# Sums of the modulation on VectorE, narrow stationary columns, and row norms by step over four tiles

## The reference

```python
# first block
mod = silu(c) @ w_ada + b_ada                     # (1, 6*1024)
shift1, scale1, gate1, shift2, scale2, gate2 = split(mod, 6)
h = rms_norm(x, norm1_w) * (1 + scale1) + shift1
q, k, v, cb, cc, cx, iq, ik, iw = split(h @ w_in)
y = concat(rms_norm(topk_attention(q, k, v, iq, ik, iw)), rms_norm(short_conv(cb, cc, cx)))
x = x + gate1 * (y @ w_out)
h2 = rms_norm(x, norm2_w) * (1 + scale2) + shift2
x = x + gate2 * retrieval(h2)                     # 16,384 single-neuron experts
# second block
x = layer_norm(ALPHA * x + hybrid_mixer(x), ...)  # its projection has 8 columns beta, a (decay)
x = layer_norm(ALPHA * x + expert_layer(x), ...)  # 32 experts, top 2
# third block
x = x + hybrid_layer(rms_norm(x), ...)            # four attention branches and w_out
```

## Time and profile before

| what | value |
|---|---|
| three timed runs | 4040.03, 4041.31, 4035.67 us; median 4040.03 |
| the profiled execution | 4024.92 us, span 4022.9 us |
| busy: TensorE, VectorE, ScalarE, GpSimd | 3259.2, 2388.5, 1419.9, 1257.1 us |
| first mixer's first product to its end | 52.9 to 489.6 us |
| mixers' first product | 2083.39 us |
| routing: last rest, first product | 2857.04, 2857.79 us |
| third block's first product | 3553.57 us |

### The profile page before, as it was taken

The page is one execution under the profiler, slowest core; times in us unless marked ns, Lnnn a source line. Parts: engine busy times, 40 slices in busy tenths (PEclk is TensorE's granted clock), DMA queues, the critical chain, the costliest instruction groups (busy, mean ns, idle before and its releaser), DMA issues. The chain is left out here.

```text
span 4022.9 us, 35798 instructions
## 1 busy us (share of the span) xinstructions
PE 3259.2 (81%) x12074; PEld 2065.8 (51%) x12074; DVE 2388.5 (59%) x4585; ACT 1419.9 (35%) x2251; POOL 1257.1 (31%) x1107
## 2 busy tenths in 40 slices
PE   8999688677666776667678898899399999578888
PEld 5555573222222222222256686677288888456556
DVE  3665474666666666666527646544489889544444
ACT  2323222112221112111114323233378888533443
POOL 0000046777777777777720000000111221100000
PEclk9999799999999999989979998799699999879888
DMA  6233178999999999999952220022599999611111
GB/s 221 66 112 103 49 244 320 355 365 367 359 361 371 361 361 369 371 362 349 371 194 76 59 73 17 27 76 93 199 338 375 373 368 375 226 42 48 32 32 53
DMA packets 421241, 896.43 MB, mean 223 GB/s; under 512 B 38081, under 2 KB 179137, under 8 KB 420418
## 3 DMA queue, kind: packets, MB, share of 16 engines
q0 software_dynamic: 157984, 549.57, 36.5%
q1 hardware_dynamic: 263074, 344.54, 25.3%
HBM read 891.80 MB, written 27.35 MB: 228 GB/s over the span
## 5 line engine op out<-in xcount | busy, mean ns | idle before, releaser
L263 PE MATMUL peer_acc<-peer_vbuf,peer_diag 128*128 128x512 f32 x2048 | 1026.1, 637 | 402.8 <-issue 181.6
L263 PEld LDWEIGHTS peer_acc<-peer_vbuf,peer_diag 128*128 128x128 f32 x2048 | 377.1, 199 | 1049.0 <-issue 897.3
L452 DVE CUSTOM_DVE_ANT_0 peer_junk<-peer_ubuf,firsts_h 128x1024 f32<-128x1024 f32 x512 | 624.7, 1225 | 452.6 <-DMA peer_ubuf<-in_peer_u,peer_experts 336.7
L220 POOL DMA_INDIRECT peer_ubuf<-in_peer_u,peer_experts x512 | 532.7, 1040 | 699.4 <-DVE peer_experts L423 533.8
L228 POOL DMA_INDIRECT peer_vbuf<-in_peer_v,peer_experts x512 | 581.5, 1136 | 230.2 <-issue 125.7
L329 ACT ACTIVATE peer_diag<-all_consts,peer_weights 128x128 f32<-128x128 f32 x512 | 194.5, 398 | 1014.2 <-PE peer_acc L263 469.4
L2985 DVE TENSOR_TENSOR slotted_low<-slotted_raw,slotted_high 128x2048 fp32r<-128x2048 f32 x192 | 434.2, 2289 | 66.1 <-ACT slotted_high L2934 66.1
L2934 ACT ACTIVATE slotted_high<-slotted_raw 128x2048 fp32r<-128x2048 f32 x192 | 365.6, 1920 | 71.1 <-PE slotted_h L2891 51.3
L2752 POOL MEMSET slotted_xg<- 128x4096 f32 x1 | 3.5, 3512 | 774.5 <-POOLq L60 774.5
L2891 PE MATMUL slotted_h<-slotted_high,slotted_xT_high 128*128 128x512 f32 x512 | 205.1, 401 | 6.2 <-DVE slotted_low L2985 4.1
L2891 PE MATMUL slotted_h<-slotted_high,slotted_xT_low 128*128 128x512 f32 x512 | 201.9, 394 | 0.0
(11 more groups left out here) (736 smaller groups left out, 5928.2 us busy)
## 6 DMA issues: line engine op xcount, KB each, us to landing
slotted_raw<-in_moe_w SPq DMA_DIRECT2D x192, 1024.0 KB, 9.2
mixers_raw<-in_w_in SPq DMA_DIRECT2D x56, 512.0 KB, 3.8
firsts_ada_raw<-in_w_ada SPq DMA_DIRECT2D x64, 256.0 KB
third_raw<-in_w_in SPq DMA_DIRECT2D x30, 512.0 KB, 3.7
firsts_raw<-in_w_in SPq DMA_DIRECT2D x28, 512.0 KB, 4.1
firsts_ada_first<-in_w_ada SPq DMA_DIRECT2D x8, 1024.0 KB
peer_s<-in_peer_wq SPq DMA_DIRECT2D x16, 512.0 KB
peer_ubuf<-in_peer_u,peer_experts POOLq DMA_INDIRECT x512
```

The source lines that it names most:

```text
L220: pool.indirect_dma_start(ubuf[:, n % R, :], None, A["peer_u"], bass.IndirectOffsetOnAxis(ap=experts[:, t, m:m + 1], axis=0))\
L263: mm = nc.tensor.matmul(acc[t % 2][j][:, :], diag[:, n % 4, :], vbuf[:, n % R, j * BANK:(j + 1) * BANK], start=(n == t * E), stop=(n == (t ...
L452: nc.vector.tensor_tensor_reduce(junk[:, n % 2, :], ubuf[:, n % R, :], h2[:, t, :], 1.0, 0.0, ALU.mult, ALU.add, act_in[:, t, m:m + 1]).th ...
```

## The change

1. **First mixer, sums.** The 64 matmuls at L687 go. VectorE multiplies each tile of `w_ada` by its column of silu(c) and adds it up (64 operations of 128x512), and one matmul with a matrix of ones sums the partitions, eight in all. Half of the 64 steps have keys from -4 on (2.25 apart), half from 140 on (2.6 apart).
2. **First mixer, plan.** Other periods for the pieces of v, q and k, and the convolution; the two closing pieces of the convolution's part are split off and come earlier, and half 1's products of a tile are cut in two; scores and softmax works have shorter spacing, selection rounds a longer one; the transposes and splits of the tail stand later.
3. **Mixers, ab.** Beta and decay columns are stationary, the 512 tokens move: 24 matmuls in place of 96, the result is copied by ScalarE and turned by four small transposes in the middle of piece 1.
4. **Routing rows.** Ordered by step over the four tiles by a written list; the norm is two operations with two tensor sources each in place of one with one source and two with two; the router's rounding and rest come after the first rows.
5. **Third block's rows.** The same order and norm; the GpSimd addition is gone, VectorE makes `x*ALPHA + ya` and then `+ yb`.

```diff
-                (stationary("v", W[:, 2 * DA:3 * DA], 4) + stationary("q", W[:, 0:DA], 4)
-                 + stationary("k", W[:, DA:2 * DA], 4), 6.9),
+                (stationary("v", W[:, 2 * DA:3 * DA], 4), 9.0),
+                (stationary("q", W[:, 0:DA], 4) + stationary("k", W[:, DA:2 * DA], 4), 6.0),
                 (stationary("cc", W[:, 4 * DA:5 * DA], 4) + stationary("cx", W[:, 5 * DA:6 * DA], 4)
-                 + stationary("cb", W[:, 3 * DA:4 * DA], 4), 11.0),
-                (closing, 5.6)]
+                 + stationary("cb", W[:, 3 * DA:4 * DA], 4), 8.0),
+                (closing[0:2], 8.0), (closing[2:], 5.6)]
...
+            now += {"2": 18.0, "0": 26.0}.get(part_of(part), 0.0)
...
-        ADA_AT, ADA_STEP = 112.0, 2.5
+        FIRST = 32
 
         def ada_key(q):
-            return ADA_AT + ADA_STEP * q
+            return 2.25 * q - 4.0 if q < FIRST else 140.0 + 2.6 * (q - FIRST)
+
+        def ada_acc(j):
+            return (acc_first if j < 4 + FIRST // 8 else acc_last)[:, j % 2, :]
...
-            for q in range(8 * (N_ADA - 4)):
-                yield ada_key(q)
-                j, k = 4 + q // 8, q % 8
-                if q == 0:
+            for j in range(4, N_ADA):
+                yield ada_key(8 * (j - 3) - 1) + 1.5
+                if j == 4:
                     pe.wait_ge(h_low, 2 * NT)
...
-                mm = nc.tensor.matmul(side[j % 2][:, :], c_col[:, k:k + 1].broadcast_to([P, P]), ada_raw[:, q % 2, :],
-                                      start=(k == 0), stop=(k == KD - 1))
+                if j >= 4 + FIRST // 8:
+                    pe.wait_ge(sq_rooted, 2)
+                pe.wait_ge(ada_out, j - 1)
+                pe.wait_ge(ada_used, 8 * (j - 3))
+                nc.tensor.matmul(side[j % 2][:, :], C["ones"], ada_acc(j), start=True, stop=True).then_inc(ada_done, 1)
...
+                    for k in range(KD):
+                        q = 8 * (j - 4) + k
+                        yield ada_key(q)
+                        dve.wait_ge(ada2_in[q % 2], 16 * (q // 2 + 1))
+                        if k == 0:
+                            dve.wait_ge(ada_done, j - 1)
+                            if q == FIRST:
+                                dve.wait_ge(rectified, len(rels))
+                            ins = nc.vector.tensor_scalar(ada_acc(j), ada_raw[:, q % 2, :], c_col[:, k:k + 1], None, ALU.mult)
+                        else:
+                            dve.wait_ge(ada_used, q)
+                            ins = nc.vector.scalar_tensor_tensor(ada_acc(j), ada_raw[:, q % 2, :], c_col[:, k:k + 1], ada_acc(j),
+                                                                 ALU.mult, ALU.add)
+                        ins.then_inc(ada_used, 1)
+                    yield ada_key(8 * (j - 3) - 1) + 4.0
...
-                return starts[IN] + 10.0 + 3.0 * (p - HALF1)
+                return starts[IN + 2] + (-8.0, -4.0, 3.0, 6.0)[p - HALF1]
...
+                    if i == 2:
+                        yield starts[HALF1] + 5.6 * t + 2.8
...
-        REL_AT, REL_STEP = done_key("iw", 0) + 3.0, 1.9
-        PICK_AT, PICK_STEP = REL_AT + REL_STEP * len(rels) + 2.0, 3.2
+        REL_AT, REL_STEP = done_key("iw", 0) + 3.0, 1.35
+        PICK_AT, PICK_STEP = REL_AT + REL_STEP * len(rels) + 2.0, 3.6
...
-                at += (3.6, 4.4, 5.0, 5.6)[t]
+                at += (3.2, 3.6, 4.2, 4.6)[t]
...
+                low_at = half1_key(t) + (11.6, 11.6, 11.6, 7.6)[t]
                 later += [(half1_key(t), 1, t), (half1_key(t) + 2.6, 2, t), (half1_key(t) + 3.2, 3, t),
-                          (half1_key(t) + 7.4, 4, 2 * t), (half1_key(t) + 7.8, 4, 2 * t + 1)]
+                          (low_at, 4, 2 * t), (low_at + 0.3, 4, 2 * t + 1)]
...
+                high_at = half1_key(t) + (9.6, 9.6, 8.6, 7.0)[t]
+                later += [(half1_key(t) + 1.6, 1, t), (half1_key(t) + 2.9, 2, t), (high_at, 3, 2 * t),
+                          (high_at + 0.4, 3, 2 * t + 1)]
...
-                yield half1_key(t) + 6.4 + 0.4 * half
+                yield half1_key(t) + (8.35, 8.35, 6.4, 6.4)[t] + 0.02 * half
...
                     if name == "ab":
-                        for t in range(NT):
-                            for k in range(KD):
-                                for r, (a, b) in enumerate(three_products((xh[:, k, tile(t)], xl[:, k, tile(t)]),
-                                                                          (wh[:, k, :], wl[:, k, :]))):
-                                    mm = nc.tensor.matmul(bank[:, 2 * BH * t:2 * BH * t + 2 * BH], a, b,
-                                                          start=(k == 0 and r == 0), stop=(k == KD - 1 and r == 2))
+                        for k in range(KD):
+                            for r, (a, b) in enumerate(three_products((xh[:, k, :], xl[:, k, :]), (wh[:, k, :], wl[:, k, :]))):
+                                mm = nc.tensor.matmul(bank[0:2 * BH, :], b, a, start=(k == 0 and r == 0),
+                                                      stop=(k == KD - 1 and r == 2))
...
+                                if p == 1:
+                                    pe.wait_ge(ab_copied, 1)
+                                    for t in range(NT):
+                                        tr = nc.tensor.transpose(big[0][:, 2 * BH * t:2 * BH * t + 2 * BH], abT[0:2 * BH, tile(t)],
+                                                                 C["ident"][0:2 * BH, 0:2 * BH])
+                                    tr.then_inc(ab_turned, 1)
...
-        later = [(row_key(t, step), step, t) for t in range(NT) for step in (2, 5, 9, 10)]
+        order = (("mean", 0), ("mean", 1), ("norm", 0), ("mean", 2), ("norm", 1), ("mean", 3), ("norm", 2), ("low", 0), ("low", 1),
+                 ("norm", 3), ("low", 2), ("low", 3), ("low", 4), ("low", 5), ("low", 6), ("low", 7))
+        for i, (what, t) in enumerate(order):
+            yield float(i)
+            if what == "mean":
...
-            elif step == 5:
+            elif what == "norm":
                 dve.wait_ge(rooted, t + 1)
                 if t == 0:
                     dve.wait_ge(rows_loaded, 32)
                 chain(nc.vector.reciprocal(roots[:, t:t + 1], roots[:, t:t + 1]))
-                chain(nc.vector.tensor_scalar(x[:, t, :], x[:, t, :], means[:, t:t + 1], roots[:, t:t + 1], ALU.add, ALU.mult))
-                chain(nc.vector.tensor_tensor(x[:, t, :], x[:, t, :], ob[:, 0, :], ALU.mult))
-                nc.vector.tensor_tensor(x[:, t, :], x[:, t, :], ob[:, 1, :], ALU.add).then_inc(x_ready, 1)
+                chain(nc.vector.scalar_tensor_tensor(x[:, t, :], x[:, t, :], means[:, t:t + 1], ob[:, 0, :], ALU.add, ALU.mult))
+                nc.vector.scalar_tensor_tensor(x[:, t, :], x[:, t, :], roots[:, t:t + 1], ob[:, 1, :], ALU.mult, ALU.add)\
+                  .then_inc(x_ready, 1)
...
-        yield -20.0
+        yield 9.5
...
-        def rows_pool(pool):
...
-                nc.gpsimd.tensor_tensor(ya[:, t, :], ya[:, t, :], yb[:, t, :], ALU.add).then_inc(y_added, 1)
...
+            order = (("add", 0), ("add", 1), ("mean", 0), ("add", 2), ("mean", 1), ("norm", 0), ("add", 3), ("mean", 2), ("norm", 1),
+                     ("second", 0), ("mean", 3), ("norm", 2), ("second", 1), ("low", 0), ("low", 1), ("norm", 3), ("second", 2),
+                     ("low", 2), ("low", 3), ("second", 3), ("low", 4), ("low", 5), ("low", 6), ("low", 7))
+            for i, (what, t) in enumerate(order):
...
+                if what == "add":
+                    dve.wait_ge(y_in[t], 32)
+                    nc.vector.scalar_tensor_tensor(ya[:, t, :], x[:, t, :], ALPHA, ya[:, t, :], ALU.mult, ALU.add)\
+                      .then_inc(y_added, 1)
                     dve.wait_ge(y_added, t + 1)
-                    nc.vector.scalar_tensor_tensor(x[:, t, :], x[:, t, :], ALPHA, ya[:, t, :], ALU.mult, ALU.add)\
-                      .then_inc(x_added, 1)
-                elif step == 3:
+                    nc.vector.tensor_tensor(x[:, t, :], ya[:, t, :], yb[:, t, :], ALU.add).then_inc(x_added, 1)
```

139 lines of the change are left out of this document (66 added, 73 removed).

## The result

The changed kernel takes 3965.28 us (median of 4 executions, 3961.64 to 3967.69) against 4037.85 (median of 4, 4031.35 to 4041.31) for the kernel before: a ratio of 0.9821 with an interval of 0.9804 to 0.9838, 73 us less. The forecast was 107 less. Direction, range and three of the four terms hold; term 1, the first mixer, gave about a third of what was forecast.

The account below looks back on a forecast made before the run. TensorE's queue was taken to set the first mixer up to 375 us, latencies between engines after it. Terms -63, -14.5, -15 and -15 sum to -107.5 from a median of 4040.03: 3932.5, rounded to 3934 us, range 3910 to 3972.

Parts of the forecast that it names:

- term 1: First mixer: modulation sums leave TensorE, its queue 53.7 us shorter; with waits, closing products and tail -63 us, bounds -30 and -80.
- Net waits, +5: First mixer: new waits of +12 us less 7 regained at the softmax's end, net +5, bounds 0 and +30.
- New order of scores and product: First mixer's softmax end: next head's scores issued before this one's product, taking back 7 of 11.7 us waited for exponentials.
- Closing products, -9: First mixer: 48 closing matmuls of the convolution's part go between softmax works, leaving 19 us behind it instead of 28.
- Tail, -5: First mixer's tail: rests placed behind the next norm remove VectorE's 5.09 us wait for rounded transposes, -5 us.
- Term 2: Mixers' beta and decay columns: 24 matmuls instead of 96, -14.5 us, bounds -9 and -16.
- Term 3: Routing rows: earlier first mean -6.7, closer tiles -6.7, shorter last norm 1.4; -15 us, bounds -11 and -18.
- Rival C: Routing: its gain is swallowed by the weight stream; total -92, 3948 us; chance 0.06.
- Term 4: Third block's rows: 37.6 us against 52.5, -15 us, bounds -10 and -17.
- A: First mixer: VectorE becomes the bound, term 1 only about -30, total -75, 3965 us; chance 0.20.
- B: Clock stays low where fillers go: 18 us come back in tile four's eight works, total -84, 3956 us; chance 0.10.
- D: First mixer: modulation steps block VectorE for whole transfer rounds, 173 us; total +65, 4105 us; chance 0.02.

Follow-up runs that it names:

- run 2: Kernel before, in its own order, with 56 of the 64 modulation matmuls and their loads left out: 3881.9 against 3885.71 us, ratio 0.9986.
- run 6: Changed kernel with the modulation sums back on TensorE, new plan kept: 3977.74 us against 4032.48 for the kernel before, ratio 0.9875.
- run 3: Changed kernel with 56 of VectorE's 64 modulation steps and their loads left out: 3811.6 us against 3885.71 for the kernel before, ratio 0.9815.
- run 9: Changed kernel with each work's product ahead of the next scores in tiles 3 and 4: 3841.16 us against 3888.96 for the kernel before, ratio 0.988.
- run 7: Changed kernel with the convolution's two closing pieces back behind the softmax: 3959.69 us against 4032.48 for the kernel before, ratio 0.9816.
- run 4: Changed kernel with 84 useless fp32r matmuls added between 224 and 345 us: 3822.79 us, ratio 0.9854 to the kernel before.
- run 8: Changed kernel with four useless matmuls before the transposes of each of the last six softmax works: 3951.23 us against 4032.48 before, ratio 0.9802.
- run 5: Changed kernel again, without an edit: 3961.65 us against 4032.48 for the kernel before, ratio 0.9813.
- run 10: Changed kernel, convolution's closing pieces back behind the softmax, four useless matmuls in each of the last eight works: 3809.42 us against 3888.96 before, ratio 0.9794.
- run 1: Kernel before with all of the change's first mixer (sums, plan, tail) and nothing else: 3858.02 against 3885.71 us, ratio 0.9938.
- run 12: Changed kernel with four useless matmuls in each of the last six softmax works, measured again: 3959.82 us against 4032.82 before, ratio 0.982.

## Why the prediction was right or wrong

**Bound of the stage (half right).** "TensorE's queue sets this stage up to 375" was read from 142.93 busy of 145.40 us. TensorE was busy, but the chain behind it was not TensorE's: with 56 matmuls less (run 2) half 1 began 2.4 us earlier. A work's chain (scores, exponentials, transposes, product) set the time, and the sums filled its gaps. The share of busy time could not show it; the place of the sums, between the transposes and the product of one work, could have.

**Term 1, the 53.7 us (wrong: this is the step that failed).** "I count it whole because TensorE is the one that is waited for in most of the stage." Alone they are worth 2.4 us (run 2), with the new plan 18 to 24 (run 6 against the two courses of the change). Of 56 us less work, 16.5 turned into waits and 23 into a lower clock. Half 1 came 42 us later than forecast, and these are the 23 of the clock, for which the sum had nothing, 11.5 of waits beyond the 5, and the 9 of the closing products, less the 2 by which the work shrank more than forecast.

**Net waits, +5 (undersized).** Measured +16. But the causes named for it (late weight rests +6, rectified scores +3, transfers +3) together are small: TensorE waited 2.9 us for a rest, and taking 56 of the 64 modulation steps out of VectorE gave 1 to 6 us (run 3). The wait at L1247, for the scaled keys, had its like before (5.5 and 1.5 us at L1225). By the windows 9 of the 16 are in the softmax, where the 7 us taken back were expected, and 4 in the closings, whose first products now come before the rest they need (L867, 3.06 us at 427.23).

**New order of scores and product, "I take 7 back" (undersized by more than half).** Run 9 gives 16 for the fourth tile, where alone the order is new. It was costed by the 11.7 us waited before, but those were what was left with fillers in place; the wait that it has to cover is the one that opens when the fillers go (33.5 + 5.7 in run 2).

**Closing products, -9 (wrong: nothing gained).** Run 7 without the move is 2 us faster, which one profile each does not tell from zero. The step that failed is that they "go between softmax works, where TensorE otherwise waits": 11 us of them made the softmax 8 us longer, and only 6.4 were saved behind it.

**Tail, -5 (right).** 39.5 to 33.0, and VectorE's wait of 5.09 us is gone.

**Term 2, -14.5 (right; profiled -9).** The 24 matmuls took 8.3 us, from 2068.01 to 2076.31 (7.9 forecast), and the row after ran at 1.00. Over eleven profiles with the change's mixers the stretch from first to last product had a mean of 649.2 us, over three with the old ones 662.1: -12.9. The profiled one gave 4 back by chance: after equal waits of 3.42 us at L1952 the matmuls came at the lower clock (2.08), where before they took 1.12.

**Term 3, -15 (right in the sum, two of its parts by luck).** -16. From the memset to the first norm it is 5.0 us less (11.8 to 6.8), not 6.7: the start was held up (last section). The tiles follow at 3.15 us, not the 4.6 taken, which gives 11.0 instead of 6.7. The last tile, from its norm to the router's product, takes 6.6 us where it took 6.8, so the 1.4 of the shorter norm did not come. VectorE is busy for 19.31 of 22.90 us, but in some 2.9 of them it was held up. Rival C did not show: router's product to experts' first is 36.4 us against 36.9.

**Term 4, -15 (right).** -17, the window 35.8 where 37.6 was worked out, VectorE busy 32.31 where 33.1 was.

**Its signs.** Half 1 was to start near 392 and the stage to end near 427; they came at 434 and 467. VectorE was busy over 240 us, as said (277), and TensorE idle in the selection for 9 us (13 forecast). Of the two signs of being wrong, the waits for weight rests stayed at 2.9 us, far under 20, and the waits for transfers passed 10 without being the cause (run 3).

**Rivals.** The time fell on A's number, 3965, but not by A's mechanism, and that the number fits is luck: VectorE was busy 277 of 414 us, and run 3 shows that its load costs 1 to 6 us, not 30. More than half of what took term 1 down is B's mechanism, the clock that falls when the fillers go. It was given 0.10 and 18 us in eight works; it ran through the whole stage from the selection on and cost 23, and the waits came on top. By the Trainium skill, "TensorE: Matmul & The Clock Gate", section "HAM oscillation — how this bites in real kernels", bursts of matmuls that are parted by waits for transfers begin slow each time. That the clock falls where fillers go and rises where they come, runs 2, 4 and 8 show, with 0.57, 1.00 and 1.00 against 0.89, 0.91 and 0.77 in the compared stretches. But not every wait does it: the works of run 8 are parted by waits of 0.40 us and run at 1.00, and after equal waits of 1.83 us one course was slow and the other not. D did not occur: VectorE's waits for the tiles came to 13.4 us in 14 times and 1.4 in three more, not 173, and two buffers were enough.

**Still open.** What decides the two courses (334 or 328 us) on equal instructions was not found: the clock after the wait at L1253 makes up most of the difference, but why it falls in one and not in the other no run shows. Of six profiles whose instructions are the change's up to 300 us, four have 0.83 from 163 to 224 us (the change, runs 5, 7 and 10) and two 0.89 (runs 1 and 9). Whether the new order in the old spacing of the works would have done with fewer waits was not tried.

## What to carry to other kernels

An engine at 98% busy is not the bound if part of its work only fills the waits of a chain: before counting removed work whole, take it out by itself, and look at whether the works end earlier. In this kernel TensorE's fillers cost next to nothing, because they stood in waits and kept the clock up, so their removal paid only together with an order that closes the gaps (here the next scores ahead of this product). Before work is moved into a gap, look at whether the chain there waits or is itself made of slow matmuls: the closing products of term 1 met the second. Where gaps must stay in a short chain at the end of a stage, a few cheap matmuls in the gap can make the chain shorter than it is without them (runs 8, 10 and 12).

## What the runs showed of the hardware

A memset by GpSimd held up VectorE's smallest operations, at the start of the routing rows. VectorE's timeline of the change:

```profile
2795.05 0.09 DVE L2686 MEMSET slotted_pad<- 128x32 f32 x1
2795.17 2.90 DVE L2688 COPY slotted_facts<-all_consts 128x4 f32<-128x4 f32 x1
2795.25 2.83 DVE L2689 TENSOR_SCALAR slotted_facts<-all_consts 128x4 f32<-128x4 f32 x1
...
2795.73 2.37 DVE L2600 TENSOR_SCALAR slotted_means<-slotted_sums 128x1 f32<-128x1 f32 x2
```

GpSimd's in the same stretch:

```profile
2794.53 3.51 POOL L2788 MEMSET slotted_xg<- 128x4096 f32 x1 [765.29 <-POOLq L60]
```

All of them end when the memset does, at about 2798.1. A mean (L2600) takes 2.37 us for two where one takes 0.15 later. VectorE's own memset of 0.09 us at 2795.05 was not held. Before, the same memset (2818.74, 3.51 us) met only memsets of VectorE, and the same copy, behind it, was short:

```profile
2818.74 3.51 POOL L2752 MEMSET slotted_xg<- 128x4096 f32 x1 [774.52 <-POOLq L60]
...
2826.79 0.17 DVE L2655 COPY slotted_facts<-all_consts 128x4 f32<-128x4 f32 x1
```

ScalarE's next pass needs the mean:

```profile
2798.25 1.15 ACT L2631 ACTIVATE slotted_squares<-all_x,slotted_means 128x1024 f32<-128x1024 f32 x1 [1.38 <-issue]
```

The Trainium skill, "SBUF — State Buffer", section "Who interferes with whom", describes a pair of ports that VectorE and GpSimd share, which one instruction holds alone until it ends; the rows agree, and they show it for copies of four elements. The 2.68 us row of the third block, which ran while GpSimd added, fits too: it ended at 3512.04, GpSimd's last addition at 3511.50. Its place in the norm is now taken by operations of 1.28 us with no GpSimd work beside them. Moving the memset by 4 us would, by my estimate, give back up to the 1.38 us for which ScalarE stood idle before that pass; it was not tried.

Extra matmuls in TensorE's waits can cost less than their own time, or gain: 19 us of them cost 6 to 10 us in the profiled first mixer (run 4), and six times 0.93 us gained 5.5 (run 8), with the clock at 1.00 instead of 0.77.
